# The low part of each weight tile on GpSimd instead of VectorE, in the GLA stage of a hybrid decoder step

## The reference

```python
h = _rmsnorm(x, ln_g)
z = h @ w_in
fq, fk, fv, ff, fg, gq, gk, gv, glr, gg, ma, mb = jnp.split(z, SPLIT_POINTS, axis=-1)
...
s_past = jnp.einsum('bqhd,bkhd->bhqk', q, k_past).astype(jnp.float32) * FOX_SCALE
...
att = jnp.where(causal, jnp.einsum('bhtd,bhsd->bhts', q_in, k_in), 0.0)
o = jnp.einsum('bhts,bhsv->bhtv', att, vc) + jnp.einsum('bhtd,bhdv->bhtv', q_in, S)
...
m = jax.nn.sigmoid(ma) * a + jax.nn.sigmoid(mb) * b
return x + m @ w_out
```

## Time and profile before

| | |
|---|---|
| median of 3 runs | 1650.24 us (1646.68 to 1652.56) |
| the profiled execution | 1644.44 us, of it the span 1642.8 us |
| TensorE busy | 1532.9 us (93%) |
| VectorE busy | 671.9 us (41%) |
| ScalarE busy | 603.4 us (37%) |
| GpSimd busy | 501.7 us (31%) |
| mean granted TensorE clock | 0.981 |

### The profile page before, as it was taken

The page is one execution under the profiler, slowest core; times in us unless marked ns, Lnnn a source line. Parts: engine busy times, 40 slices in busy tenths (PEclk is TensorE's granted clock), DMA queues, the critical chain, the costliest instruction groups (busy, mean ns, idle before and its releaser), DMA issues.

```text
span 1642.8 us, 33880 instructions
## 1 busy us (share of the span) xinstructions
PE 1532.9 (93%) x11281; PEld 1262.4 (77%) x11281; DVE 671.9 (41%) x1498; ACT 603.4 (37%) x1287; POOL 501.7 (31%) x952
## 2 busy tenths in 40 slices
PE   5989899998979998999999999999998899999988
PEld 5878787786768776788777887678875688888876
DVE  4444353635434444634445434454354223332221
ACT  5344444444533344324443334533344354111100
POOL 4444434420072134333343333453331123111000
PEclk9999999998989999999999999999999999999999
DMA  4131212122156566776676766777664655222521
GB/s 170 31 84 32 82 44 82 31 63 66 42 168 193 160 196 221 229 221 209 200 235 216 256 205 206 227 236 223 203 205 156 215 214 178 93 94 93 161 90 58
DMA packets 146909, 249.96 MB, mean 152 GB/s; under 512 B 37513, under 2 KB 52362, under 8 KB 146226
## 3 DMA queue, kind: packets, MB, share of 16 engines
q1 hardware_dynamic: 115154, 215.78, 41.8%
q0 software_dynamic: 31584, 32.02, 6.4%
HBM read 217.47 MB, written 30.22 MB: 151 GB/s over the span
## 4 chain that ended last, share of the span: by engine, by line
PE 58%; DMA 4%; ACT 3%; DVE 3%; issue 2%; SPq 1%; POOL 0%; DVEq 0%; ACTq 0%
PE psum L288 24%; PE psum L1895 7%; PE psum L2356 6%; PE psum L1910 4%; PE psum L2348 4%; PE psum L1943 3%; PE psum L2386 3%; DMA w_raw<-in_w_tiles 2%; PE psum L2016 1%; PE psum L2026 1%; DMA v_page<-in_cache_v 1%; PE psum L2023 1%; PE psum L1926 1%; PE psum L1986 1%; PE psum L2395 1%
## 5 line engine op out<-in xcount | busy, mean ns | idle before, releaser
L288 PE MATMUL psum<-h_hi,w_hi 128*128 128x384 f32 (+1 forms) x1344 | 495.3, 368 | 17.9 <-issue 12.9
L288 PE MATMUL psum<-h_hi,w_lo 128*128 128x384 f32 (+1 forms) x1344 | 447.2, 333 | 0.0
L288 PE MATMUL psum<-h_lo,w_hi 128*128 128x384 f32 (+1 forms) x1344 | 446.0, 332 | 0.0
L1465 POOL DMA_DIRECT2D sc<-tmp_bias x512 | 252.6, 502 | 309.0 <-PE psum L1926 306.0
L288 PEld LDWEIGHTS psum<-h_hi,w_hi 128*128 128x128 f32 x1344 | 258.1, 192 | 96.2 <-issue 91.2
L288 PEld LDWEIGHTS psum<-h_lo,w_hi 128*128 128x128 f32 x1344 | 259.3, 193 | 2.4
L288 PEld LDWEIGHTS psum<-h_hi,w_lo 128*128 128x128 f32 x1344 | 257.5, 192 | 0.0
L674 POOL DMA_DIRECT2D lfp<-in_cache_logf x256 | 124.1, 485 | 176.1 <-issue 176.1
L1895 PE MATMUL psum<-con,k_page 128*128 128x128 f32 x1024 | 152.5, 276 | 9.6 <-DVE k_t L1395 6.4
L1514 ACT ACTIVATE k_t<-psum 128x512 f32<-128x512 f32 x128 | 76.1, 595 | 186.9 <-PE psum L1895 186.9
L1895 PEld LDWEIGHTS psum<-con,k_page 128*128 128x128 f32 x1024 | 120.9, 141 | 30.3 <-issue 26.2
(11 more groups left out here) (262 smaller groups left out, 2176.1 us busy)
## 6 DMA issues: line engine op xcount, KB each, us to landing
k_page<-in_cache_k SPq DMA_DIRECT2D x256, 256.0 KB, 3.7
v_page<-in_cache_v SPq DMA_DIRECT2D x256, 256.0 KB, 3.1
w_raw<-in_w_tiles SPq DMA_DIRECT2D x63, 512.0 KB, 4.9
g_pair<-tmp_gates SPq DMA_DIRECT2D x16, 544.0 KB, 4.6
sc<-tmp_bias POOLq DMA_DIRECT2D x512, 16.0 KB, 2.9
tmp_ogla<-gate POOLq DMA_DIRECT2D x4, 1088.0 KB, 5.2
g_pair<-tmp_ogla SPq DMA_DIRECT2D x8, 544.0 KB, 8.0
x_in<-in_x_prompt SPq DMA_DIRECT2D x8, 512.0 KB, 6.1
```

The source lines that it names most:

```text
L288: m = pe.matmul(out, wt[:, s, k, :], h[:, k, t0:t0 + w], start=(k == 0 and a == 0), stop=(k == KT_ - 1 and a == 2))
L1465: pool.dma_start(sc[r0:r0 + TS, j % SLOTS, :], src.to_broadcast([TS, 512])).then_inc(sc_in[j % SLOTS], 16)
```

## The change

`split_lo` of the GLA stage's 34 tiles is called by GpSimd's program instead of VectorE's, at the same step. The other stages are as they were.

```diff
@@ -1500,7 +1500,11 @@
-            run(pool, {"prep": prep, "vn_load": vn_load, "att": att_step, "satt": satt, "sstate": sstate, "ev_z": gate_out, "end": end})
+            def z(n, c, part):
+                if c == 0 and part == 1:
+                    stream.split_lo(pool, n)
+
+            run(pool, {"z": z, "prep": prep, "vn_load": vn_load, "att": att_step, "satt": satt, "sstate": sstate, "ev_z": gate_out, "end": end})
@@ -1757,10 +1761,6 @@
-
-            def z(n, c, part):
-                if c == 0 and part == 1:
-                    stream.split_lo(dve, n)
@@ -1878,7 +1878,7 @@
-                      "decay": decay, "dec_last": dec_last, "dec_diff": dec_diff, "z": z, "evac": evac, "ev_y": ev_y, "ev_z": ev_z, "att": att_step,
+                      "decay": decay, "dec_last": dec_last, "dec_diff": dec_diff, "evac": evac, "ev_y": ev_y, "ev_z": ev_z, "att": att_step,
```

## The result

The changed kernel took 1664.4 us in the median of 6 runs (1660.6 to 1669.1), against 1649.7 us (1646.7 to 1652.6) for 6 runs of the kernel before beside them: a ratio of 1.009, with a 95% interval of 1.0069 to 1.011. It is 14.7 us slower, and 1664.4 us lies within the range given and 1.6 us under the forecast.

A forecast was written before the change was run, and what follows sets the result against it. TensorE's written order was taken as the bound. A 19.3 us hold plus 2.0 us of clock less 5.5 us of relief gave +15.8 us, 1660.2 for the profiled execution, 1666 as median; range 1654 to 1676.

The forecast's parts named there:

- The first hold: Head of the stage: first `w_lo` queues behind GpSimd's 64 bias DMAs, so TensorE stands still for 13.9 us.
- The second part: Just after the first hold: late key pages and a half-rate clock add 4.8, 0.6 and 2.0 us.
- the page: Head of the stage: sixth key page's reload, behind the delayed weight load, arrives late, 3.7 to 5.8 us, taken as 4.8.
- the pair: Key pages after the sixth: 0.6 us more for the pair that stood together.
- the clock: After the long idle time at the stage's head, TensorE runs at half rate: 2 us lost, bounds 0 and 4.
- The relief: TensorE's waits behind VectorE's `w_lo` shrink: 5.5 us gained, bounds 2 and 12.
- The five waits: TensorE's waits for `o_n` (four) and `att` (one) behind a VectorE `w_lo`: 7.8 us to gain at most.
- The steady part: After the stage's start: slower GpSimd subtractions and delayed bias tiles still arrive in time, price 0, cover 8 us.
- Blocking: Rival: two-SBUF-input VectorE instructions are held by GpSimd's `w_lo`; up to 16 us more, 1682; chance 8%.
- A relief larger than the hold: Rival: all TensorE waits for VectorE go, with clock 26.7 us against 21.3; 5.4 us faster, 1645; chance 3%.
- late in the steady part: Rival: GpSimd's queue also delays five later tiles by 4 us each; 20 us more, 1686; chance 4%.
- swallowed: Rival: page reloads or last value pages set the end, so hold minus relief stays within 0.3%, 1650; chance 6%.

The follow-up runs named there:

- the pair of kernels that split them from the rest: Kernel before with only subtractions 6, 7, 23, 31, 32 on GpSimd: 0.9968; with only the other 28 there, subtraction 0 on VectorE: 0.9993.
- part 3: Kernel before, all 34 subtractions on VectorE but moved to the last quarter of the tile's first chunk: 1638.3 us, 0.9933.
- the five waits alone: Kernel before with only subtractions 6, 7, 23, 31, 32 moved to GpSimd: 0.9968, 5.3 us faster.

## Why the prediction was right

*The first hold: 13.9 us said, 13.6 measured.* The queue (31.53 us said, 31.51 measured) plus one subtraction (2.4 us, from `o_lo` scaled to its columns; 2.38 measured) against the time at which TensorE wanted the tile. Three kernels confirm the mechanism: without the queue no hold, with three quarters of it 5.8 us, and with the other 33 subtractions back on VectorE 13.8 us.

*The second part: 4.8 for the page, 0.6 for the pair and 2.0 for the clock said, 7.4 us; 5.8 us measured up to tile 2.* The sum was near, the parts less so. The page wait that shows is 2.25 us, under the 3.7 to 5.8 that I had bounded it by, for two reasons of about the same size. TensorE crept through its matmuls at the half rate and wanted the page 2.3 us after the hold instead of 1.1. And the page was there 4.5 us after the hold instead of 5.9: its reload took 3.5 us from issue to use, not the 4.8 or so that I had put between its own median and the weight loads' longest. The other 3.5 us of the second part are the half rate, above the 2.0 taken and inside its bounds of 0 and 4; where no page is late it is 2.4. No wait for the second page of the pair shows. The whole hold was priced at 21.3 us. By the traces it is 19.7 us in both kernels that have it, 1.6 us less. By the times it comes out at 22.3 and 24.1, with the clock of four to twelve runs in them.

*The relief: 5.5 us said, 7.6 us measured* (5.1 to 10.2 by the interval of the kernel with subtraction 0 on VectorE), *and 4.2 at equal clock.* The working had 7.8 us as the most and took off 2.3 for waits that might turn into waits for pages. In the trace of after, `o_n` and `att` fall by 7.7 us together, as the most had it. What grew against them has these rows in the kernel before, from 500 to 1345 us:

```profile
PE psum L1943 <- DMA v_page<-in_cache_v: 5.7, 8, 1.4
...
PE psum L2023 <- DVE state L1835: 1.8, 2, 1.2
```

The waits for value pages went from 5.7 to 7.8 us, 2.1 more, close to the 2.3 taken off. But they are 8.0 us also where the 28 other subtractions are on GpSimd and `o_n` is as before, so the growth cannot be put down to the relief by one trace of each kernel. The waits for `state` went from 1.8 to 3.4 us; the 1.57 us behind a blocked mask I had not priced within the forecast. The five waits are the right ones, by the pair of kernels that split them from the rest.

*The steady part: price 0 said.* Confirmed: no TensorE wait for `w_lo` after the first, and none with 2.4 us more on each, under the 8 us of cover read from the tightest tile.

*The rivals.* Blocking was priced at 16 us if a third of the windows met the masks or the decay chain. The mechanism is in the trace of the changed kernel, with 6.2 us on VectorE and 1.57 us on TensorE. The `kdec` difference and a `gate` product were named; a second `gate` product and the mask were missed. One sign of being wrong was thus met once: a two-input instruction stretched to 2 us with TensorE waiting behind it, at a tenth of the rival's price. A relief larger than the hold did not come; it needed 21.3 us and was 7.6. The queue is not late in the steady part. The hold is not swallowed: 13.5 us at tile 1, 19.3 at tile 2 and 20.6 at the end.

In part the closeness is luck, whichever way one counts: by the times hold and relief were each 1 to 3 us larger than said, by the traces and at equal clock each was 1 to 2 us smaller, and in a difference the two errors cancel.

## What to carry to other kernels

An instruction that moves to another engine takes its place in that engine's order, and what it costs is decided at the one place where that order is fullest, here 64 DMA issues ahead of the first of 34, and not by its own duration or by the engine's share. Then look who else waits for the same result: a load that waited for it held back page reloads that did not need it, for 3.4 us more. And where a result is late because another instruction stands ahead of it, try first to move that instruction further back in its own engine's order: two parts later on VectorE gave 0.9933 (0.9909 to 0.9957), where the move to GpSimd gave 1.009.

## What the runs showed of the hardware that was not expected

- A VectorE instruction with both inputs in SBUF that met a GpSimd subtraction ended 0.15 us after it (a mask, 1918 ns against 292), 0.35 us after it (a `gate` product, 1752 against 492) or 1.09 us after it (the `kdec` difference, 3600 against 1220, though it had started 0.11 us before the subtraction). With two subtractions back to back it got through between them, so in these rows the hold lasted one pass at most. An instruction with one input in PSUM was not touched.
- After 13.6 us without work TensorE got the half rate from 496 to 506 us. In the first 5 of these it was busy for 2.35 us only, since it waited for a page. Where the pages were there it got the half rate from 497.7 to 503 us. A wait of 5.8 us was followed by the half rate as well, from 489 to 499 us, with a page late by 3.1 us.
- A bias row's DMA takes 0.49 us of GpSimd's own order (64 in 31.51 us, 48 in 23.75 us), so a subtraction of 2.4 us behind them waits 13 times its own length.
- Open: moving `w_lo` to part 3 gave 11 us (ratio interval 0.9909 to 0.9957) where the five waits alone gave 5.3 (0.9951 to 0.9986). The waits for `o_n` and `att` are the same in both. At equal clock the difference is 2.4 us (6.9 less 4.5), with about 2.1 either way, and of that I can point only to what is absent, the blocking: the waits for `state` sum to 2.0 us instead of 3.4. How much of the rest is real isn't settled.
